# Two sets of raw-weight buffers in a dense FFN, and partition sums by block transpose, row sum and a narrow product

## The chip, the cores and the metric

The kernel runs on 1 core of one Trainium2 chip. The metric is the device time of one execution in microseconds (us). Before the change the median of 3 runs is 1362.73 us (1361.41 to 1363.16).

## What is computed

Two layers over 256 latent tokens of width 1024. Layer 0 is windowed attention (with 256 context tokens as extra keys) and a dense SwiGLU FFN; layer 1 is a pooling mixer and a top-2-of-8 expert FFN. Each sub-layer takes shift, scale and gate vectors from adaLN, a vector-matrix product with a large matrix:

```python
def ada_mod(cond, w, b):
    m = jax.nn.silu(cond) @ w + b
    return jnp.split(m[..., None, :], 6, axis=-1)

def swiglu(h, w_gu, w_down):
    g, u = jnp.split(h @ w_gu, 2, axis=-1)
    return (jax.nn.silu(g) * u) @ w_down

h = modulate(rmsnorm(x, g_pre_ffn), sh_f, sc_f)
f = swiglu(h, ffn_w_gu[slot], ffn_w_down[slot])
x = x + gt_f * rmsnorm(f, g_post_ffn)
```

All is float32. `D_MODEL` is 1024, `D_FF` 2816, `D_FF_EXPERT` 3584.

## The kernel before

The program is written engine by engine; each engine runs its own list in order and waits on semaphores.

**The dense FFN** goes through its 2816 inner columns in 11 steps of 256 (`FSTEPS`, `FS`). A step has three raw weight tiles of 1 MB: f_raw0 and f_raw1 (gate and up columns for the first and the second half of the 1024 inputs) and f_raw2 (256 rows of the down matrix). SyncE (SP) asks for them in `dense_step`. To multiply in full precision each raw tile is split: ScalarE writes a rounded copy f_hi (`dense_hi`, L1177), VectorE the rest f_lo = f_raw - f_hi (`dense_lo`, L1548). TensorE runs per step `gate_up` (48 matmuls on three pairs of parts, L823 to L825), the turn of the last step's activations (L856), one `column_sums` (L660), and `down` of the last step (24 matmuls, L871). In iteration `st` ScalarE does: turned activations of st-1, f_hi0 of st+1, SiLU of st, f_hi1 of st+1, f_hi2 of st. VectorE does: fT_lo of st-1 (L1580), f_lo0 of st+1, the gate product f_act (L1589), f_lo1 of st+1, f_lo2 of st, `take_columns`, and an adaLN piece (`sum_piece`). f_hi and f_lo have one buffer for each of the three kinds, so f_hi2 is written when `down` has read it (semaphore f_used2).

Before the change f_raw too has one buffer for each kind. SP asks for a step's tile when VectorE has split the last step's (f_split0 to f_split2), and its waits stand in one line: f_raw0 and f_raw1 of the next step come behind f_raw2 of this one.

**adaLN.** The matrices have 24 pieces of 512 columns. After the first four, a piece is taken by VectorE: with rows on partitions it scales and adds eight 128x512 chunks into ada_acc (L1414, L1417, `sum_chunk`), which leaves 128 partial sums for each column. `column_sums` adds them up over the partitions on TensorE: four products with a 128-column block of ada_acc as the stationary operand and one column of ones as the moving one, each two records in the profile. `take_columns` (L1408) adds the bias. Pieces 0 to 5 (`MIXER_PIECES`) are taken during the projections; 6 to 9 during attention, a chunk per head on VectorE, and TensorE takes the column sums at heads 10, 18, 26 and after the last; from 10 (`EARLY`) on, one piece in each FFN step 0 to 9, so that its column sums come in the next. GpSimd asks for the pieces.

**Attention** goes over 32 heads-and-blocks `u`: TensorE computes scores of u (L733 to L735), turns the probabilities of u-2 (L744) and weighs the values of u-3 (L755); VectorE takes the maximum (L1510), ScalarE the exponential (L1145).

**The experts' stage** (TensorE L1029 and L1043) begins after the pooling mixer and the router. SP loads its weights (`load`, L410) into five 28 KB-per-partition buffers that begin at SBUF offset R0, where q_parts and the raw FFN tiles lie before.

Of the kernel before, what the change touches and what calls it, by code (L numbers as in the profile page):

```python
# [44 lines left out]
FF = 2816  # L45
FS = 256
# [6 lines left out]
UNIT = 32  # L53
# [80 lines left out]
def build(nc, x, c, ctx_in, c_ctx, ada_w, ada_b, norm_g, w_qkv, w_o, sink, pool_w, pool_b, pool_scale,  # L134
# [4 lines left out]
    def sb(name, shape, dt, at):  # L139
        return nc.alloc_sbuf_tensor_at(name, [shape[0], *shape[1:]], dt, offset=base + at)  # L140
# [155 lines left out]
    def bank(i):  # L296
        return ps[:, i, :]

    names = """x_in ctx_in wqkv_in0 wqkv_in1 wqkv_in2 consts_in tr2_hi mask_r_ready ada_summed ada_rows_taken rows_in sink_in rb_in wo_in ada_in0 ada_in1 ada_in2 ada_fourth_in ada_late_in
        pool_in cols_turned cols_ready silu_ready ada_used acc_ready colsum_ready mod_ready a_ready nsink_ready  # L300
# [4 lines left out]
        f_in0 f_in1 f_in2 f_split0 f_split1 f_split2 f_hi0 f_hi1 f_hi2 f_used0 f_used1 f_used2  # L305
        f_silu f_act_ready f_turned f_thi f_tlo hf_hi_ready hf_ready
# [50 lines left out]
    def _(sp):  # L357
# [18 lines left out]

        def dense_step(st):

            for k in range(2):
                if not isinstance(st, int):  # L380
                    sp.wait_ge(s[f"f_split{k}"], st)
                for half, at in ((0, 0), (1, FF)):
                    sp.dma_start(f_raw[k][:, :, half * FS:half * FS + FS],
                                 gu_v[:, 4 * k:4 * k + 4, bass.ds(st * FS + at, FS)]).then_inc(s[f"f_in{k}"], 16)
            if not isinstance(st, int):
                sp.wait_ge(s["f_split2"], st)
            sp.dma_start(f_raw[2][:], dn_v[bass.ds(st, 1)].rearrange("a p q n -> p (a q) n")
                         if not isinstance(st, int) else dn_v[st]).then_inc(s["f_in2"], 16)
# [206 lines left out]
    def _(pe):  # L595
# [472 lines left out]
    def _(act):  # L1068
# [96 lines left out]

        def dense_hi(k, st):

            act.wait_ge(s[f"f_in{k}"], (st + 1) * (32 if k < 2 else 16))
            if k == 2 and isinstance(st, int) and st == FSTEPS - 1:
                act.wait_ge(s["f_used0"], FSTEPS)  # L1170
                act.activation(last_hi[:], f_raw[k][:], ACT.Copy).then_inc(s["f_hi2"], 1)
# [5 lines left out]
            act.activation(f_hi[k][:], f_raw[k][:], ACT.Copy).then_inc(s[f"f_hi{k}"], 1)  # L1177

        load_table(ACT.Sqrt, 4)
        dense_hi(0, 0)  # L1180
        for b in range(TB):
            act.wait_ge(s["wo_ready"], 2 * b + 2)
            y = ps[:, 3 + 2 * b:5 + 2 * b, :]
            if b == 1:
                act.wait_ge(s["y_normed"], 1)
            squares(NORM_Y + 2 * b, [(y, y_tmp[:].rearrange("p (a n) -> p a n", a=2))])
            root(NORM_Y + 2 * b)
            if b == 1:
                dense_hi(1, 0)
# [21 lines left out]

        def dense_iteration(st, first=False, last=False):
            if not first:
                dense_turned_hi(st - 1)
            if not last:
                dense_hi(0, st + 1)
            dense_silu(st)
            if not last:
                dense_hi(1, st + 1)
            dense_hi(2, st)  # L1220

        dense_iteration(0, first=True)
        with act.Fori(1, FSTEPS - 1) as st:
            dense_iteration(st)
        dense_iteration(FSTEPS - 1, last=True)
        dense_turned_hi(FSTEPS - 1)

# [102 lines left out]
    def _(dve):  # L1330
# [17 lines left out]
        def inverse_root(n):  # L1348
# [61 lines left out]
        def sum_chunk(q, w, k):  # L1410

            v, acc_q = cols[:, N_SC + 2 * k:N_SC + 2 * k + 1], acc_of(q)
            if k == 0:
                ins = dve.tensor_scalar(acc_q[:], w[:, k, :], v, None, ALU.mult)  # L1414
            else:
                dve.wait_ge(s["acc_ready"], q * KC + k)
                ins = dve.scalar_tensor_tensor(acc_q[:], w[:, k, :], v, acc_q[:], ALU.mult, ALU.add)  # L1417
            ins.then_inc(s["acc_ready"], 1)

        def sum_piece(q, w):  # L1420
            for k in range(KC):
                sum_chunk(q, w, k)
# [84 lines left out]
        for u in range(NU):  # L1507
# [35 lines left out]

        def dense_lo(k, st):
# [54 lines left out]
        dense_iteration(0, first=True)  # L1599
        with dve.Fori(1, FSTEPS - 1) as st:  # L1600
            dense_iteration(st)
        dense_iteration(FSTEPS - 1, last=True)
        dense_turned_lo(FSTEPS - 1)
# [246 lines left out]
```

## Time and profile before

| | before |
|---|---|
| median of 3 runs | 1362.73 us |
| the profiled execution, its own time | 1363.89 us |
| its span, first to last instruction | 1362.2 us |
| TensorE busy | 1210.1 us, 89% |
| VectorE busy | 579.1 us, 43% |
| ScalarE busy | 315.5 us, 23% |
| mean granted TensorE clock | 0.955 |
| bytes moved | 461.20 MB, 339 GB/s over the span |
| dense FFN, first to last matmul | about 220 to 430 us |
| experts' first matmul | 489.65 us |

Busy times are unions over the span. PE is TensorE's matmuls, PEld its weight loads, DVE VectorE, ACT ScalarE, POOL GpSimd, SP SyncE. A busy TensorE in the profile is one with a matmul in its pipeline.

### The profile page before, as it was taken

To read this page: it belongs to the slowest core of one execution; us is meant where nothing else is said; L and a number is where in the kernel's file an instruction comes from. 1 tells how busy PE (TensorE), PEld (TensorE's weight loads), DVE (VectorE), ACT (ScalarE), POOL (GpSimd) and SP (SyncE) were. 2 spreads that over 40 slices of the span, in tenths; PEclk is the share of its full clock that TensorE was granted. 3 is DMA by queue.
4 is the path that set the end of the run, shared out by engine and by line. 5 is a ranking of instruction groups with operands and counts; after the bars stand their busy time and mean duration, and the time that the engine had idled before them with its cause. 6 is when DMAs were issued, how large, how long until landed. Compare 5 with 4: busy or idle time off the path is not lost.

```text
span 1362.2 us, 43494 instructions
## 1 busy us (share of the span) xinstructions
PE 1210.1 (89%) x16960; PEld 850.3 (62%) x16960; DVE 579.1 (43%) x1117; ACT 315.5 (23%) x535; POOL 168.3 (12%) x517
## 2 busy tenths in 40 slices
PE   3898998999999999989979899878989976999971
PEld 1456975788888676656647566546755644766751
DVE  0597845777776543232323233312432321323322
ACT  2005653334343422111102012011111100211111
POOL 1010000000010011111111111111111110111111
PEclk9899999999999999999989899989999988999996
DMA  9995120588899458899999999999999999999995
GB/s 336 390 367 191 63 93 32 192 293 291 303 324 403 190 210 347 331 410 414 412 411 411 402 412 411 412 415 410 411 412 413 411 411 412 413 373 411 414 406 180
DMA packets 129077, 461.20 MB, mean 339 GB/s; under 512 B 8240, under 2 KB 34016, under 8 KB 120672
## 3 DMA queue, kind: packets, MB, share of 16 engines
q1 hardware_dynamic: 114368, 403.78, 75.4%
q0 software_dynamic: 13952, 55.58, 11.0%
q8 instruction: 74, 1.21, 0.4%
q10 hardware_dynamic: 672, 0.54, 0.2%
q14 instruction: 11, 0.09, 0.0%
HBM read 455.81 MB, written 4.06 MB: 338 GB/s over the span
## 4 chain that ended last, share of the span: by engine, by line
PE 66%; DMA 15%; SPq 8%; DVE 4%; issue 4%; ACT 1%; POOL 0%; POOLq 0%; DVEq 0%; ACTq 0%
PE ps L1029 28%; PE ps L1043 13%; DMA w_gu<-in_moe_w_gu 8%; SPq L410 8%; PE ps L871 4%; PE ps L695 4%; PE ps L823 2%; PE ps L824 2%; PE ps L825 2%; DMA ctx_tok<-in_ctx 2%; PE ps L813 2%; PE ps L755 2%; DMA w_dn<-in_moe_w_down 1%; DMA ada<-in_ada_w 1%; DMA f_raw<-in_ffn_w_gu 1%
## 5 line engine op out<-in xcount | busy, mean ns | idle before, releaser
L1029 PE MATMUL ps<-w_gu,x_cur 128*32 128x224 f32 x10240 | 514.0, 363 | 61.6 <-issue 29.9
L1029 PEld LDWEIGHTS ps<-w_gu,x_cur 128*32 128x32 f32 x10240 | 362.8, 113 | 209.5 <-issue 74.8
L1043 PE MATMUL ps<-w_dn,consts_sb 128*32 128x256 f32 x4480 | 258.8, 385 | 20.1 <-POOL consts_sb L548 10.1
L1761 DVE TENSOR_TENSOR cols<-cols,ps 128x224 f32<-128x224 f32 x160 | 91.7, 573 | 416.7 <-PE ps L1029 416.7
L1043 PEld LDWEIGHTS ps<-w_dn,consts_sb 128*32 128x32 f32 x4480 | 151.8, 111 | 121.0 <-issue 34.7
L1289 ACT ACTIVATE cols<-ps 128x224 f32<-128x224 f32 x160 | 93.4, 584 | 561.3 <-PE ps L1029 433.3
L1417 DVE SCALAR_TENSOR_TENSOR ada_acc<-ada,cols,ada_acc 128x512 f32<-128x512 f32 x140 | 105.0, 750 | 4.0
L1548 DVE TENSOR_TENSOR f_lo<-f_raw,f_hi 128x2048 fp32r<-128x2048 f32 x32 | 73.0, 2292 | 48.1 <-ACT f_hi L1177 46.9
L537 POOL COPY x_cur<-x_all 128x128 f32 x160 | 47.7, 298 | 317.4 <-PE ps L1029 271.0
L1177 ACT ACTIVATE f_hi<-f_raw 128x2048 fp32r<-128x2048 f32 x32 | 61.0, 1916 | 65.9 <-DMA f_raw<-in_ffn_w_gu 60.7
L823 PE MATMUL ps<-f_hi,hf_hi 128*128 128x512 f32 x176 | 71.5, 406 | 2.7 <-DVE f_act L1589 2.7
L539 POOL COPY x_cur<-x_all 128x128 f32 x160 | 47.4, 296 | 181.2 <-PE ps L1029 181.2
L824 PE MATMUL ps<-f_lo,hf_hi 128*128 128x512 f32 x176 | 69.7, 396 | 0.0
L825 PE MATMUL ps<-f_hi,hf_lo 128*128 128x512 f32 x176 | 69.6, 395 | 0.0
L1304 ACT ACTIVATE kept<-cols 128x224 f32 x80 | 31.2, 390 | 145.1 <-DVE cols L1761 145.1
L1788 DVE TENSOR_TENSOR y_all<-y_all,ps 128x256 f32 x60 | 25.3, 422 | 78.7 <-PE ps L1043 68.1
L1791 DVE TENSOR_TENSOR y_all<-y_all,ps 128x256 f32 x80 | 33.7, 422 | 56.0 <-PE ps L1043 56.0
L548 POOL COPY consts_sb<-kept 128x128 f32 x80 | 23.7, 296 | 177.7 <-DVE kept L1776 108.0
L695 PE MATMUL ps<-wqkv,hT 128*128 128x512 f32 x96 | 44.1, 613 | 1.1 <-DVE hT L1388 1.1
L823 PEld LDWEIGHTS ps<-f_hi,hf_hi 128*128 128x128 f32 x176 | 33.7, 191 | 10.6 <-issue 3.2
L513 POOL DMA_DIRECT2D ada<-in_ada_w x10 | 8.9, 885 | 251.8 <-DVE ada_acc L1417 251.8
L825 PEld LDWEIGHTS ps<-f_hi,hf_lo 128*128 128x128 f32 x176 | 33.8, 192 | 7.4
(246 smaller groups left out, 1067.6 us busy)
## 6 DMA issues: line engine op xcount, KB each, us to landing
w_gu<-in_moe_w_gu SPq DMA_DIRECT2D x256, 896.0 KB
w_dn<-in_moe_w_down SPq DMA_DIRECT2D x32, 2048.0 KB
w_dn<-in_moe_w_down SPq DMA_DIRECT2D x32, 1536.0 KB
ada<-in_ada_w POOLq DMA_DIRECT2D x23, 2048.0 KB, 10.1
f_raw<-in_ffn_w_gu SPq DMA_DIRECT2D x44, 512.0 KB, 6.7
f_raw<-in_ffn_w_down SPq DMA_DIRECT2D x11, 1024.0 KB, 4.9
wqkv<-in_attn_w_qkv SPq DMA_DIRECT2D x3, 2048.0 KB, 19.6
wo_sb<-in_attn_w_o SPq DMA_DIRECT2D x1, 4096.0 KB, 23.6
```

The lines of the kernel that those rows point to most:

```text
L410: sp.dma_start(to, src).then_inc(s[f"w_{x}{part // 2}"], 32 if kind == DOWN else 16)
L695: mm = pe.matmul(bank(3 + u % 4), src[:, k, b * P:(b + 1) * P], wqkv[:, k, 512 * n:512 * n + 512], start=(k == 0), stop=(k == KC - 1))
L823: pe.matmul(bank(1 + b), hi, f_hi[k][:, kk, :], start=first, stop=False)
L824: pe.matmul(bank(1 + b), hi, f_lo[k][:, kk, :], start=False, stop=False)
L825: mm = pe.matmul(bank(1 + b), lo, f_hi[k][:, kk, :], start=False, stop=last)
L1029: mm = pe.matmul(ps[UNIT * t:UNIT * t + UNIT, bank_, 0:W], x_cur[:, k, :], w_gu[x][:, k, W * t:W * t + W], start=(k % 4 == 0), stop=(k % 4 ...
L1043: mm = pe.matmul(ps[UNIT * t:UNIT * t + UNIT, bank_, 0:OW], act_cur[:, q, :], w_dn[x][:, q, OW * t:OW * t + OW], start=(q == rows[0]), sto ...
L1177: act.activation(f_hi[k][:], f_raw[k][:], ACT.Copy).then_inc(s[f"f_hi{k}"], 1)
L1289: act.activation(halves.rearrange("p (q c) -> p c q", q=MQ), ps[:, HALF_BANK, 0:W].rearrange("p (c q) -> p c q", q=MQ), ACT.Copy).then_inc ...
L1417: ins = dve.scalar_tensor_tensor(acc_q[:], w[:, k, :], v, acc_q[:], ALU.mult, ALU.add)
L1548: dve.tensor_tensor(lo[:], f_raw[k][:], hi[:].bitcast(F32), ALU.subtract).then_inc(s[f"f_split{k}"], 1)
L1761: dve.tensor_tensor(view, view, ps[:, REST_BANK, 0:W].rearrange("p (c q) -> p c q", q=MQ), ALU.add).then_inc(s["rest_taken"], 1)
```

## The change

1. f_raw gets two sets ("sides") of three tiles. Side 0 lies where the tiles lay, side 1 at R0, over q_parts and two small attention tiles. Step st uses side st mod 2. SP asks for step 0 as before, for step 1 when attention's output is taken (o_taken 4) and adaLN pieces to 9 are done (mod_ready), and for step st from 2 on when the tiles of step st-2 are split. Loops of SP, ScalarE and VectorE take two steps an iteration. The experts' first three quarter chunks lie under side 1 and now wait for the splits of step 9.
2. For adaLN pieces from 6 on, VectorE turns ada_acc in 32x32 blocks (`gather_rows`: transpose, then a sum over the 32 elements of each row), which leaves 4x4 values on each partition; TensorE multiplies them with a 128x32 pattern of ones (`fold_all`, made once by a row sum) in four narrow products, one for each 32 partitions of the output.

```diff
-    f_raw = [sb(f"f_raw{k}", [P, 4, 2 * FS] if k < 2 else [P, 2, D], F32, R0 + 24 * KB + 8 * KB * k)
-             for k in range(3)]
+    f_raw = [[sb(f"f_raw{k}{side}", [P, 4, 2 * FS] if k < 2 else [P, 2, D], F32, R0 + 24 * KB * (1 - side) + 8 * KB * k)
+              for side in range(2)] for k in range(3)]
...
+        def dense_step(st, side):
+            fixed = isinstance(st, int)
             for k in range(2):
+                if not fixed:
+                    sp.wait_ge(s[f"f_split{k}"], st - 1)
...
+            if not fixed:
+                sp.wait_ge(s["f_split2"], st - 1)
...
         sp.wait_ge(s["qkv_ready"], 8)
-        dense_step(0)
-        with sp.Fori(1, FSTEPS) as st:
-            dense_step(st)
+        dense_step(0, 0)
+        sp.wait_ge(s["o_taken"], 4)
+        sp.wait_ge(s["mod_ready"], EARLY)
+        dense_step(1, 1)
+        with sp.Fori(0, FSTEPS // 2 - 1) as i:
+            for side in range(2):
+                dense_step(i * 2 + (2 + side), side)
+        sp.wait_ge(s["f_split0"], FSTEPS - 2)
+        sp.wait_ge(s["f_split1"], FSTEPS - 2)
+        sp.wait_ge(s["f_split2"], FSTEPS - 2)
...
+        for k in range(3):
+            sp.wait_ge(s[f"f_split{k}"], FSTEPS - 1)
         load(0, GATE, 0, 0, (0, 1, 2))
...
         def column_sums(q):
+            if not isinstance(q, int) or q >= MIXER_PIECES:
+                pe.wait_ge(s["acc_rows_ready"], q - MIXER_PIECES + 1)
+                pe.wait_ge(s["mod_ready"], q)
+                for t in range(TILES):
+                    mm = pe.matmul(ps[UNIT * t:UNIT * t + UNIT, 0, 0:4], fold_all, acc_rows[:, t, :], start=True, stop=True)
+                mm.then_inc(s["colsum_ready"], 1)
+                return
...
+        done(dve.tensor_reduce(fold_all, ident.rearrange("p (j a) -> p a j", a=UNIT), AX.X, ALU.add), step_, wait=False)
...
+        def gather_rows(q):
+            n = q - MIXER_PIECES
+            dve.wait_ge(s["acc_ready"], (q + 1) * KC)
+            dve.transpose(acc_turned[:].rearrange("p a b -> p (a b)"), acc_of(q)[:]).then_inc(s["acc_turned_ready"], 1)
+            dve.wait_ge(s["acc_turned_ready"], n + 1)
+            dve.tensor_reduce(acc_rows[:].rearrange("p t k -> p k t"), acc_turned[:].rearrange("p (k t) b -> p k t b", t=TILES),
+                              AX.X, ALU.add).then_inc(s["acc_rows_ready"], 1)
...
+            if u % KC == 0 and u:
+                gather_rows(MIXER_PIECES + u // KC - 1)
...
+        gather_rows(EARLY - 1)
         take_columns(EARLY - 1)
...
                 sum_piece(st + EARLY, ada_ring[0])
+                gather_rows(st + EARLY)
```

VectorE at the end of FFN step 0 and the head of the next, before the change (f_lo_78 and f_lo_79 are the low parts of kinds 1 and 2):

```order
L1548 TENSOR_TENSOR f_lo_78<-f_raw_64,f_hi_75 128x2048 [waits f_hi1]
L1548 TENSOR_TENSOR f_lo_79<-f_raw_65,f_hi_76 128x2048 [waits f_hi2]
L1414 TENSOR_SCALAR ada_acc_92<-ada_70,cols 128x512 [waits ada_late_in]
L1417 SCALAR_TENSOR_TENSOR ada_acc_92<-ada_70,cols,ada_acc_92 128x512 [waits acc_ready] x7
L1600 UNCONDITIONAL_BRANCH
L1580 TENSOR_TENSOR fT_lo<-ps,fT_hi 128x512 [waits f_thi]
```

and now:

```order
L1592 TENSOR_TENSOR f_lo_81<-f_raw_66,f_hi_78 128x2048 [waits f_hi1]
L1592 TENSOR_TENSOR f_lo_82<-f_raw_67,f_hi_79 128x2048 [waits f_hi2]
L1446 TENSOR_SCALAR ada_acc_95<-ada_73,cols 128x512 [waits ada_late_in]
L1449 SCALAR_TENSOR_TENSOR ada_acc_95<-ada_73,cols,ada_acc_95 128x512 [waits acc_ready] x7
L1456 STREAM_TRANSPOSE acc_turned<-ada_acc_95 128x512 [waits acc_ready]
L1458 TENSOR_REDUCE acc_rows<-acc_turned 128x4x4 [waits acc_turned_ready]
L1624 TENSOR_TENSOR fT_lo<-ps,fT_hi 128x512 [waits f_thi]
```

The two new instructions stand between the piece's sum and fT_lo, as in every step up to the ninth.

SP's requests from the FFN's first on, before (f_raw_63 to f_raw_65 are kinds 0 to 2):

```order
L383 DMA f_raw0_63<-in_ffn_w_gu 128x4x256 [waits qkv_ready]
L383 DMA f_raw0_63<-in_ffn_w_gu 128x4x256
L383 DMA f_raw1_64<-in_ffn_w_gu 128x4x256 x2
L387 DMA f_raw2_65<-in_ffn_w_down 128x2x1024
L392 UNCONDITIONAL_BRANCH
L383 ISA [waits f_split0]
L383 DMA f_raw0_63<-in_ffn_w_gu 128x4x256
```

and now (the last digit of f_raw00 or f_raw01 is the side):

```order
L388 DMA f_raw00_63<-in_ffn_w_gu 128x4x256 [waits qkv_ready]
L388 DMA f_raw00_63<-in_ffn_w_gu 128x4x256
L388 DMA f_raw10_65<-in_ffn_w_gu 128x4x256 x2
L392 DMA f_raw20_67<-in_ffn_w_down 128x2x1024
L388 DMA f_raw01_64<-in_ffn_w_gu 128x4x256 [waits mod_ready,o_taken]
L388 DMA f_raw01_64<-in_ffn_w_gu 128x4x256
L388 DMA f_raw11_66<-in_ffn_w_gu 128x4x256 x2
L392 DMA f_raw21_68<-in_ffn_w_down 128x2x1024
L400 UNCONDITIONAL_BRANCH
```

Step 1's four requests stand ahead of the loop, behind a wait of their own.

## Rows read from the trace of the kernel before

**Rows 1.** The page's slices of the span: DMA engines' busy share in tenths.
```profile
DMA  9995120588899458899999999999999999999995
```

**Rows 2.** Chain of waits in order of time: start us, us, what.
```profile
249.86 10.97 DMA f_raw<-in_ffn_w_gu
...
489.65 10.40 PE ps L1029 x213
```

**Rows 3.** Timeline, one FFN step: start us, us, engine, line, operation, count, [idle before, releaser].
```profile
298.18 0.39 PE L823 MATMUL ps<-f_hi,hf_hi 128*128 128x512 f32 x1
...
310.76 1.92 ACT L1177 ACTIVATE f_hi<-f_raw 128x2048 fp32r<-128x2048 f32 x1 [5.90 <-DMA f_raw<-in_ffn_w_gu]
...
315.95 0.39 PE L823 MATMUL ps<-f_hi,hf_hi 128*128 128x512 f32 x1
...
316.21 1.92 ACT L1177 ACTIVATE f_hi<-f_raw 128x2048 fp32r<-128x2048 f32 x1 [0.53 <-PE ps L871]
...
318.16 2.29 DVE L1548 TENSOR_TENSOR f_lo<-f_raw,f_hi 128x2048 fp32r<-128x2048 f32 x1 [0.15 <-ACT f_hi L1177]
...
320.95 5.47 DVE L1417 SCALAR_TENSOR_TENSOR ada_acc<-ada,cols,ada_acc 128x512 f32<-128x512 f32 x7
...
327.30 0.94 PE L660 MATMUL ps<-consts_sb,ada_acc 128*128 128x1 f32 x8
...
328.11 0.72 PE L871 MATMUL ps<-f_hi,fT_hi 128*128 128x512 f32 x2
```

**Rows 4.** Timeline of FFN steps 1 to 3.
```profile
261.79 0.39 PE L823 MATMUL ps<-f_hi,hf_hi 128*128 128x512 f32 x1
...
262.80 4.49 DVE L1548 TENSOR_TENSOR f_lo<-f_raw,f_hi 128x2048 fp32r<-128x2048 f32 x2 [1.47 <-ACT f_hi L1177]
...
267.79 5.48 DVE L1417 SCALAR_TENSOR_TENSOR ada_acc<-ada,cols,ada_acc 128x512 f32<-128x512 f32 x7
...
273.40 1.05 PE L660 MATMUL ps<-consts_sb,ada_acc 128*128 128x1 f32 x8
...
280.33 0.47 PE L823 MATMUL ps<-f_hi,hf_hi 128*128 128x512 f32 x1 [0.29 <-DVE f_act L1589]
```

**Rows 5.** Timeline of attention heads 8 to 11, and of the stage's end.
```profile
138.38 0.47 PE L733 MATMUL ps<-k_hi,q_parts 128*128 128x512 f32 x1
...
140.23 0.47 PE L733 MATMUL ps<-k_hi,q_parts 128*128 128x512 f32 x1
...
142.98 0.47 PE L733 MATMUL ps<-k_hi,q_parts 128*128 128x512 f32 x1
...
143.78 0.69 DVE L1510 TENSOR_REDUCE small<-ps 128x1 f32<-128x512 f32 x1 [1.14 <-PE ps L735]
...
188.28 0.16 DVE L1408 TENSOR_TENSOR cols<-ps,cols 128x4 f32<-128x4 f32 x1 [3.84 <-PE ps L660]
```

**Rows 6.** VectorE's groups by form: count, busy us, mean ns, idle before.
```profile
L1417 DVE SCALAR_TENSOR_TENSOR ada_acc<-ada,cols,ada_acc 128x512 f32<-128x512 f32 x140 | 105.0, 750 | 4.0
...
L1774 DVE STREAM_TRANSPOSE actT<-cols 128x224 f32<-128x224 f32 x80 | 32.9, 412 | 2.7
...
L1510 DVE TENSOR_REDUCE small<-ps 128x1 f32<-128x512 f32 x32 | 22.0, 688 | 7.6 <-PE ps L735 7.4
```

**Rows 7.** Timeline of weight loads at the router's logits.
```profile
467.05 0.38 PEld L980 LDWEIGHTS ps<-hr,route_wide 128*32 128x32 f32 x16 [0.81 <-DVE hr L1682]
467.62 0.30 PEld L961 LDWEIGHTS ps<-consts_sb 128*128 128x128 f32 x2 [0.20 <-issue]
```

**Rows 8.** Timeline, TensorE at the last step's down.
```profile
424.19 0.70 PE L871 MATMUL ps<-down_last_hi,fT_hi 128*128 128x512 f32 x2 [0.84 <-ACT fT_hi L1207]
```

**Rows 9.** Timeline at step 1, and a stretch: busy us by engine, PEclk, DMA.
```profile
242.32 0.47 PE L823 MATMUL ps<-f_hi,hf_hi 128*128 128x512 f32 x1 [2.36 <-DVE f_act L1589]
...
244.00:246.00 2.00, 2.00 (x6) 1.62 (x5) 2.00 (x2) 0.19 (x1) 0.00 (x0) 0.50 0.00 0
```

More of the change, by code:

```diff
@@ L202, in build @@
     g_row = sb("g_row", [P, D], F32, S[0])
+    acc_turned = sb("acc_turned", [P, 16, 32], F32, S[0] + 4 * KB)
+    acc_rows = sb("acc_rows", [P, 4, 4], F32, S[0] + 6 * KB)
     y_tmp = sb("y_tmp", [P, D], F32, S[0] + 4 * KB)
@@ L241, in build @@
     ones = ct[:, K_ONE:K_ONE + P]
+    fold_all = cols[:, 416:416 + UNIT]
     def cos_of(b):
@@ L299, in build @@
     names = """x_in ctx_in wqkv_in0 wqkv_in1 wqkv_in2 consts_in tr2_hi mask_r_ready ada_summed ada_rows_taken rows_in sink_in rb_in wo_in ada_in0 ada_in1 ada_in2 ada_fourth_in ada_late_in
-        pool_in cols_turned cols_ready silu_ready ada_used acc_ready colsum_ready mod_ready a_ready nsink_ready
+        pool_in cols_turned cols_ready silu_ready ada_used acc_ready acc_turned_ready acc_rows_ready colsum_ready mod_ready a_ready nsink_ready
         sumsq_ready msq_ready sqrt_ready rstd_ready dve_step xn_ready turn_ready turned_taken
@@ L304, in build @@
         row_ready row_taken wo_ready y_normed
-        f_in0 f_in1 f_in2 f_split0 f_split1 f_split2 f_hi0 f_hi1 f_hi2 f_used0 f_used1 f_used2
+        f_in00 f_in01 f_in10 f_in11 f_in20 f_in21 f_split0 f_split1 f_split2 f_hi0 f_hi1 f_hi2 f_used0 f_used1 f_used2
         f_silu f_act_ready f_turned f_thi f_tlo hf_hi_ready hf_ready
@@ L375, in _ @@
         sp.dma_start(wo_sb[:], w_o[0].rearrange("(k p) n -> p k n", p=P)).then_inc(s["wo_in"], 16)
-        def dense_step(st):
+        def dense_step(st, side):
+            fixed = isinstance(st, int)
             for k in range(2):
-                if not isinstance(st, int):
-                    sp.wait_ge(s[f"f_split{k}"], st)
+                if not fixed:
+                    sp.wait_ge(s[f"f_split{k}"], st - 1)
                 for half, at in ((0, 0), (1, FF)):
[L383 to L388, printed above, removed]
@@ L390, in _ @@
-        sp.wait_ge(s["qkv_ready"], 8)
-        dense_step(0)
-        with sp.Fori(1, FSTEPS) as st:
-            dense_step(st)
+                    sp.dma_start(f_raw[k][side][:, :, half * FS:half * FS + FS],
+                                 gu_v[:, 4 * k:4 * k + 4, bass.ds(st * FS + at, FS)]).then_inc(s[f"f_in{k}{side}"], 16)
+            if not fixed:
+                sp.wait_ge(s["f_split2"], st - 1)
+            sp.dma_start(f_raw[2][side][:], dn_v[st] if fixed else dn_v[bass.ds(st, 1)].rearrange("a p q n -> p (a q) n")
+                         ).then_inc(s[f"f_in2{side}"], 16)
@@ new lines, in _ @@
+        sp.wait_ge(s["qkv_ready"], 8)
+        dense_step(0, 0)
[8 more added lines that the diff above has]
+        sp.wait_ge(s["f_split2"], FSTEPS - 2)
+        assert FSTEPS % 2 == 1
+        for k in range(2):
+            for half, at in ((0, 0), (1, FF)):
+                sp.dma_start(f_raw[k][0][:, :, half * FS:half * FS + FS],
+                             gu_v[:, 4 * k:4 * k + 4, (FSTEPS - 1) * FS + at:FSTEPS * FS + at]).then_inc(s[f"f_in{k}0"], 16)
@@ L395, in _ @@
+        sp.dma_start(f_raw[2][0][:], dn_v[FSTEPS - 1]).then_inc(s["f_in20"], 16)
         GATE, UP, DOWN = range(KINDS)
@@ L1164, in _, with dense_hi @@
         take_row(g_row, (0, 7), 0)
-        def dense_hi(k, st):
-            act.wait_ge(s[f"f_in{k}"], (st + 1) * (32 if k < 2 else 16))
+        def dense_hi(k, st, side, turn):
+            act.wait_ge(s[f"f_in{k}{side}"], (turn + 1) * (32 if k < 2 else 16))
             if k == 2 and isinstance(st, int) and st == FSTEPS - 1:
                 act.wait_ge(s["f_used0"], FSTEPS)
-                act.activation(last_hi[:], f_raw[k][:], ACT.Copy).then_inc(s["f_hi2"], 1)
+                act.activation(last_hi[:], f_raw[k][side][:], ACT.Copy).then_inc(s["f_hi2"], 1)
                 return
@@ L1176, in dense_hi @@
                 act.wait_ge(s[f"f_used{k}"], st)
-            act.activation(f_hi[k][:], f_raw[k][:], ACT.Copy).then_inc(s[f"f_hi{k}"], 1)
+            act.activation(f_hi[k][:], f_raw[k][side][:], ACT.Copy).then_inc(s[f"f_hi{k}"], 1)
         load_table(ACT.Sqrt, 4)
-        dense_hi(0, 0)
+        dense_hi(0, 0, 0, 0)
         for b in range(TB):
@@ L1210, in _, with dense_iteration @@
         take_row(g_row, (0, 7), 2)
-        def dense_iteration(st, first=False, last=False):
+        def dense_iteration(st, side, turn, first=False, last=False):
+            ahead = (1 - side, turn + side)
             if not first:
@@ L1215, in dense_iteration @@
             if not last:
-                dense_hi(0, st + 1)
+                dense_hi(0, st + 1, *ahead)
             dense_silu(st)
             if not last:
[L1219 to L1225, printed above, removed]
+                dense_hi(1, st + 1, *ahead)
+            dense_hi(2, st, side, turn)
+        dense_iteration(0, 0, 0, first=True)
+        dense_iteration(1, 1, 0)
+        with act.Fori(0, FSTEPS // 2 - 1) as i:
+            for side in range(2):
+                dense_iteration(i * 2 + (2 + side), side, i + 1)
+        dense_iteration(FSTEPS - 1, 0, FSTEPS // 2, last=True)
         dense_turned_hi(FSTEPS - 1)
@@ L1542, in y_flat, with dense_lo @@
             return v if len(v.shape) == 2 else v.rearrange("p a n -> p (a n)")
-        def dense_lo(k, st):
+        def dense_lo(k, st, side):
             dve.wait_ge(s[f"f_hi{k}"], st + 1)
             hi, lo = (last_hi, last_lo) if k == 2 and isinstance(st, int) and st == FSTEPS - 1 else (f_hi[k], f_lo[k])
-            dve.tensor_tensor(lo[:], f_raw[k][:], hi[:].bitcast(F32), ALU.subtract).then_inc(s[f"f_split{k}"], 1)
+            dve.tensor_tensor(lo[:], f_raw[k][side][:], hi[:].bitcast(F32), ALU.subtract).then_inc(s[f"f_split{k}"], 1)
         dve.wait_ge(s["row_taken"], 2)
-        dense_lo(0, 0)
+        dense_lo(0, 0, 0)
         for b in range(TB):
@@ L1555, in _ @@
             if b == 1:
-                dense_lo(1, 0)
+                dense_lo(1, 0, 0)
             inverse_root(NORM_Y + 2 * b + 1)
@@ L1581, in dense_turned_lo, with dense_iteration @@
                               fT_hi[:].rearrange("p q b t -> p (q b t)").bitcast(F32), ALU.subtract).then_inc(s["f_tlo"], 1)
-        def dense_iteration(st, first=False, last=False):
+        def dense_iteration(st, side, first=False, last=False):
             if not first:
@@ L1586, in dense_iteration @@
             if not last:
-                dense_lo(0, st + 1)
+                dense_lo(0, st + 1, 1 - side)
             dve.wait_ge(s["f_silu"], st + 1)
@@ L1590, in dense_iteration @@
             if not last:
-                dense_lo(1, st + 1)
-            dense_lo(2, st)
+                dense_lo(1, st + 1, 1 - side)
+            dense_lo(2, st, side)
             if not first:
@@ L1597, in dense_iteration @@
                 sum_piece(st + EARLY, ada_ring[0])
[L1599 to L1602, printed above, removed]
+                gather_rows(st + EARLY)
+        dense_iteration(0, 0, first=True)
+        dense_iteration(1, 1)
+        with dve.Fori(0, FSTEPS // 2 - 1) as i:
+            for side in range(2):
+                dense_iteration(i * 2 + (2 + side), side)
+        dense_iteration(FSTEPS - 1, 0, last=True)
         dense_turned_lo(FSTEPS - 1)
```

2 lines of the change are left out of this document (1 added, 1 removed).

## The prediction

> **What bounds the kernel now.** I read the page's slices first. From the eighteenth slice on the DMA engines stand at nine tenths and more [rows 1]: that is the experts' stage, which streams 3.67 MB chunks through five buffers as TensorE frees them. Nothing of it is edited. Its first buffers fill long before TensorE arrives, and each later load waits for a freed buffer, so a stage before it that ends 1 us sooner moves TensorE's start, the freeing and the last byte 1 us sooner. I count whatever happens before 489 us at full value.
>
> The chain of waits in order of time comes next, for the dense FFN between 220 and 430 us. It runs through a raw-weight DMA of 10.97 us near 250 us, and reaches the experts' first matmul at 489.65 [rows 2]. So a late raw tile is on the path early in this stage; whether it is in its steady part is for the timeline.
>
> Step to step the first `gate_up` matmul goes from 298.18 to 315.95: 17.77 us. ScalarE does wait 5.90 us for raw weights before its copy at 310.76 [rows 3], which is the wait that the change is to remove, but TensorE has no gap. The step is TensorE's own sum: column sums start at 327.30, 11.35 us after the step's start; `down` starts 0.81 us later, and the next step 5.61 us after that [rows 3].
>
> Beside it runs a second round that nearly closes too. When `down` has read f_hi2, ScalarE refills it (316.21, 0.26 us after the step's start), VectorE splits it (318.16) and then sums the adaLN piece until 320.95 + 5.47 = 326.42, which is 10.47 us into the step [rows 3]. Only then may TensorE take the column sums. Released in 0.13 us (267.79 + 5.48 = 273.27, matmul at 273.40 [rows 4]) this round would allow 10.60 us; TensorE arrives at 11.35. **The slack is 0.75 us**, and the second part of the change puts two VectorE instructions into just this round.
>
> **The change, part by part.** *Raw weights in two sets.* The same bytes move through the same queue: each step SP still issues five DMAs when f_split2 lets it go, but for tiles needed one step later. ScalarE's f_hi0 copy will follow the turned activations at once, up to 5.90 us earlier. Steady gain for TensorE: 0, since it did not wait. f_hi2 does not move: it waits for `down`, not for data. SP now waits for o_taken and mod_ready before step 1's loads; behind it stand only FFN loads, and they go out near 190 us, when the DMA is nearly idle, and are used after 237. The experts' first three quarter chunks wait for the splits of step 9 (side 1 lies under them). In the order of the rows that is the very split that released them before: 0. The last step's raw `down` comes earlier, but TensorE there waits 0.84 us for ScalarE's turned activations [rows 8], so 0. If this cover went, the price would be 0.84 us at most.
>
> *What VectorE gains as work.* A block transpose of 512 columns and a row sum of 512. The transpose is in the trace with 224 columns at 0.412 us, the row sum with 512 (from PSUM) at 0.688 [rows 6]. VectorE's slope is (2.29 - 0.75) / 1536 = 1.0 ns per column (f_lo with 2048 columns [rows 3], the adaLN step with 512 [rows 6]), so the transpose is 0.412 + 0.29 = 0.70. Dependent instructions follow each other after 0.04 us (seven adaLN steps of 0.75 take 5.47). Together 0.04 + 0.70 + 0.04 + 0.69 = **1.47 us**. Bounds: 1.2 (row sum from SBUF cheaper) and 2.0 (it takes its 4x4x32 view more slowly). I take the middle, as both rows are of the same engine and nearly the same shape.
>
> *What TensorE loses as work.* Four products with a 128-column stationary operand, eight records, 0.81 us between neighbours here [rows 3] and 0.90 in attention: a head that has them takes 142.98 - 140.23 = 2.75 us, one that has not 140.23 - 138.38 = 1.85 [rows 5]. The new ones have a 32-column stationary operand and four moving columns. The router's logits are the nearest rows: 16 such loads in 0.38 us, about 0.02 each, then 0.20 us of idle before the next full-width load [rows 7]. So 8 x 0.02 + 0.20 = **0.38 us** from the first to `down`. The entry into the narrow form is in no row free of other waits: 0 to 0.20; I take 0.17, 0.55 in all where TensorE arrives without a wait. The Trainium skill (TensorEngine Tiling (Array Packing), Key Properties) says that changing the tiling mode, not just the tile, drains TensorE. By this rule the way out costs the 0.20 us that the row shows, in the sum above; without it the products would be 0.16 us everywhere and the change some 3 us better.
>
> *Attention, pieces 6 to 9.* Four column sums, 0.90 - 0.55 = 0.35 us each. The fourth stands in front of the last VectorE chain of the stage, which waits 3.84 us for it [rows 5], so all four count: **-1.4 us** (bounds -2.6 and 0). VectorE's 1.47 us fall behind heads 8, 16 and 24. VectorE idles 1.14 us before the maximum of the head whose scores stand behind the column sums [rows 5], with less before each head until then, and the probabilities are turned two heads after their scores, 3.7 us. This covers 1.47 us barely; if the cover were gone, up to 0.5 us each, 1.5 in all.
>
> *FFN, beginning.* Step 1's column sums find the sums ready, so 0.26 us is saved and step 2 starts at 261.53 instead of 261.79 [rows 4]. In step 2 f_hi1 was late for want of raw weights, and f_lo2 with it (262.80 x2, 4.49 us to 267.29). Now f_lo2 ends at 261.53 + 0.26 + 1.92 + 0.03 + 2.29 = 266.03 and the sum 5.98 later at 272.01; column sums at 272.01 + 1.47 + 0.13 = 273.61, step 3 at 273.61 + 0.38 + 5.61 = 279.60. It was 280.33 [rows 4]: **-0.7 us**. This is all that the second buffer set earns.
>
> *FFN, steady.* Column sums start at 10.47 + 1.47 + 0.13 = 12.07 us into the step. Plus 0.38 and 5.61: 18.06, against 17.77: +0.29 a step. Over the seven steps from 3 to 10 and the column sums of step 10, 8 x 0.29 = **+2.3 us**. Behind the new pair on VectorE stand fT_lo (`down` needs it about 0.9 us into its run; it ends 0.7 us after the pair), f_lo0 and f_act, which end some 3 us after that (0.7 + 2.29 + 0.7 after the pair's 11.94), at 15.6 of 18.06. None is late.
>
> *Start.* One more row sum, 128 columns, while VectorE idles: 0.
>
> **Sum:** -1.4 - 0.7 + 2.3 = +0.2 us. The profiled execution's own 1363.89 us becomes 1364.1. It lay 1.2 us above the median of the three runs, so against 1362.73 I predict **1362.9 us**. A measurement of this kernel can tell about 0.2%, 2.7 us, from no change.
>
> **Rivals.**
> A. *The VectorE round sets the step* (above): 1362.9, own range 1360.5 to 1365.5. Chance 0.56.
> B. *The narrow products cost next to nothing*: 0.20 in all. Attention -2.8, beginning -1.1, step 12.07 + 0.20 + 5.61 = 17.88, +0.9 in eight: -3.0, so 1359.7. For it: 0.02 us a load [rows 7]. Against: the 0.20 us of idle in the same rows. Chance 0.14.
> C. *TensorE stays the bound.* If the pair took under 0.75 us, or f_hi2 came sooner, the step would be 17.77 - 0.43 = 17.34: -3.4, with attention and beginning -5.5, so 1357.2. Against: f_hi2 hangs on `down`, and the row sum's row alone is 0.69. Chance 0.06.
> D. *Slower: the VectorE round is longer than I sum.* It decides from about 1.8 us for the pair on, since each 0.1 us costs 0.8. The likeliest way is a row sum that takes two slots of 1.0 ns for each of its 512 columns, as it walks them in short rows: 0.51 us more, a pair of 1.98, a step of 18.57, 8 x 0.51 = 4.1 us more, +4.3 in all, so 1367.0. For it: no row has such a view or a row sum of this width from SBUF. Against: VectorE's rows of 512 and 2048 columns keep one slope. Chance 0.18. The Trainium skill (VectorE: DVE Perf Modes, The DRAIN you can't avoid) names another way: a flush behind each operation of its duration less 266 ns, which would put an estimated 0.43 us behind the transpose and give 1366.3. The trace speaks against that one, with seven adaLN steps of 0.75 us that follow each other after 0.04 [rows 3, 6].
> E. *TensorE's clock falls at the new wait* of 12.07 - 11.35 = 0.7 us a step. After TensorE's idle 2.36 us before 242.32 the granted clock was 0.50 from 244 to 246, that is 1.2 GHz [rows 9]; 2 us at half speed lose 1, in every step 8 us, 1371. Against: the wait of 0.84 us at 424.19 [rows 8] was followed by two matmuls in 0.70 us, no more than the 0.72 at 328.11 [rows 3]. Chance 0.03.
> F. *The buffers don't do what they say*, f_hi0 still late: the beginning gains nothing, 1363.6. Chance 0.03; the SP rows speak against it.
>
> **The numbers.** 1362.9 is A's. Faster by over 0.2% (below 1360.0): C, most of B, an edge of A: 0.20. Slower by over 0.2% (above 1365.4): most of D, E: 0.18. Same: 0.62. The range of 1359.0 to 1367.0 holds A, B and most of D; C and E stay out.
>
> **What would show it.** ScalarE's wait for raw weights, 5.90 us in the step shown, gone but for the last step; TensorE waiting 0.6 to 0.8 us in each FFN step for acc_rows; a steady step of 18.0 to 18.1; transpose 0.70 and row sum 0.69 us; heads with column sums at 2.4 instead of 2.75 us; the first experts' matmul within 1 us of 489.65. I am wrong if the step is under 17.8 (B, C) or over 18.3 (D, E), or if a head after a VectorE pair is late.

## The result, and the profile after

| | before | changed |
|---|---|---|
| median of 20 runs each, same chip | 1363.59 us | 1361.62 us |
| ratio, 95% interval | | 0.9983 (0.9975 to 0.9991) |
| profiled execution, own time and span | 1363.89, 1362.2 us | 1361.92, 1360.2 us |
| TensorE, VectorE busy | 1210.1, 579.1 us | 1201.8, 596.2 us |
| experts' first matmul | 489.65 us | 487.56 us |

The change gains 0.17%, 2.3 us with an interval of 1.2 to 3.4. The forecast was 0.2 us of loss, so it is off by 2.5 us and wrong in sign. That the median lies in the range of 1359.0 to 1367.0 says little: the range is 8 us wide and holds no change at all. A ratio is always to runs of the kernel before on the same chip; other tables compare single executions by their traces.

One FFN step of the changed kernel, from its timeline (start us, us, engine, line, operation, count, idle before), answers to [rows 3]:

```profile
313.97 1.92 ACT L1204 ACTIVATE f_hi<-f_raw 128x2048 fp32r<-128x2048 f32 x1 [4.12 <-PE ps L898]
...
324.22 0.71 DVE L1456 STREAM_TRANSPOSE acc_turned<-ada_acc 128x512 f32<-128x512 f32 x1
324.97 0.69 DVE L1458 TENSOR_REDUCE acc_rows<-acc_turned 128x16 f32<-128x512 f32 x1
...
325.57 0.68 DVE L1624 TENSOR_TENSOR fT_lo<-ps,fT_hi 128x512 fp32r<-128x512 f32 x1
...
325.79 0.24 PE L678 MATMUL ps<-acc_rows,cols 128*32 128x4 f32 x8 [0.56 <-DVE acc_rows L1458]
...
325.96 0.73 PE L898 MATMUL ps<-f_hi,fT_hi 128*128 128x512 f32 x2
```

This step starts at 313.71 and the next at 331.56: 17.85 us. ScalarE now waits for TensorE (4.12 us), no longer for raw weights. The pair takes 0.71 and 0.69 us. TensorE waits 0.56 us for it and takes the products 12.08 us into the step. From there to `down` are 0.17 us. (The profile counts the 0.56 us from where it shows the last matmul ending. That one starts at 324.84 and the next would start 0.23 us later, at 325.07, so the products come 0.72 us later than they could.)

The table of waits of the changed kernel, 215 to 440 us (engine, line, waited for: us, times, longest):

```profile
PE ps L678 <- DVE acc_rows L1458: 4.9, 9, 0.6
...
ACT f_hi L1204 <- DMA f_raw<-in_ffn_w_gu: 3.8, 2, 3.2
```

In the kernel before ScalarE waited 60.7 us, 18 times, for raw gate and up weights here. The first line is the new wait: nine times 0.5 to 0.6 us. The last line is step 9, where ScalarE waits for the last step's weights.

Attention's head with column sums, in TensorE's timeline, and the end of the stage on VectorE, answer to [rows 5]:

```profile
140.53 0.47 PE L760 MATMUL ps<-k_hi,q_parts 128*128 128x512 f32 x1
...
142.51 0.24 PE L678 MATMUL ps<-acc_rows,cols 128*32 128x4 f32 x8
142.68 0.50 PE L760 MATMUL ps<-k_hi,q_parts 128*128 128x512 f32 x1
...
186.29 0.16 DVE L1440 TENSOR_TENSOR cols<-ps,cols 128x4 f32<-128x4 f32 x1 [1.73 <-PE ps L678]
```

Such a head takes 142.68 - 140.53 = 2.15 us instead of 2.75, so the sums cost 0.30 us over a plain head's 1.85. VectorE's chain at the end starts 1.99 us sooner.

**Where the time went.** Cut at five places of TensorE's timeline, for nine of the runs (us, as differences of starts; the steps by their first `gate_up` matmul):

| run | first head to FFN | FFN to step 2 | step 2 to 3 | mean of next 7 | step 10 to experts |
|---|---|---|---|---|---|
| before | 96.65 | 41.31 | 18.54 | 17.79 | 84.82 |
| before_again | 96.67 | 39.68 | 17.85 | 17.82 | 84.72 |
| changed | 94.37 | 41.71 | 17.85 | 17.83 | 84.68 |
| after_again | 94.38 | 40.75 | 17.83 | 17.83 | 84.67 |
| e1_buffers | 96.64 | 39.68 | 17.76 | 17.76 | 84.67 |
| e2_sums | 94.71 | 40.58 | 19.01 | 17.85 | 84.71 |
| e3_sums_after_down | 94.37 | 40.61 | 17.27 | 17.27 | 83.92 |
| e4_both_later | 94.36 | 40.63 | 17.21 | 17.20 | 83.84 |
| e8_later_one_raw_set | 94.38 | 41.09 | 19.25 | 17.55 | 83.97 |

Changed less before: -2.28, +0.40, -0.69, 7 x 0.045 = +0.32 and -0.14; the first head was 0.30 later. Together -2.09 us, as at the experts' first matmul. The two profiled once more differ by -2.29, +1.07, -0.02, +0.12, -0.05. Only the first column is stable: attention earns 2.3 us. The second and third vary with the execution, and the rest is some tenths. The second column's higher numbers are no cost of the change: e6 and e7 (below), which have its buffers and its sums, take 39.44 and 39.58 us there, no more than the 39.68 of before_again.

### The profile page after: what moved, and what is told of

Same layout as the page of the kernel before. It is cut to its first block, busy times and chain, and to the rows that moved or that the text cites. A ratio compares the mean times of both kernels' runs of the same rounds, so it can differ in the third digit from the quotient of the medians.

```text
span 1360.2 us, 43450 instructions
## 1 busy us (share of the span) xinstructions
PE 1201.8 (88%) x16960; PEld 841.1 (62%) x16960; DVE 596.2 (44%) x1146; ACT 314.7 (23%) x535; POOL 166.8 (12%) x517
## 4 chain that ended last, share of the span: by engine, by line
PE 60%; DMA 11%; DVE 10%; SPq 10%; issue 6%; ACT 2%; DVEq 0%; POOL 0%; POOLq 0%; ACTq 0%
PE ps L1056 28%; PE ps L1070 12%; SPq L428 9%; DMA w_gu<-in_moe_w_gu 6%; PE ps L898 5%; PE ps L722 4%; DVE ada_acc L1449 4%; PE ps L840 2%; PE ps L782 2%; DMA wqkv<-in_attn_w_qkv 2%; DMA w_dn<-in_moe_w_down 1%; ACT f_hi L1204 1%; DMA ada<-in_ada_w 1%; PE ps L771 1%; PE ps L760 1%
```

## The experiments

**Each part alone, and each kernel once more.** e1 is the changed kernel with the old column sums for all pieces:

```diff
-            if not isinstance(q, int) or q >= MIXER_PIECES:
+            if False:
```

and without its three `gather_rows` calls and `fold_all`.

> The kernel before with the two sets of raw buffers alone; the column sums of all pieces stay as they were. Theory (the buffers earn only the late raw tile of the second step): steady step 17.77 us as before, step 2 starts at 261.79, step 3 at 261.79 + 17.77 = 279.56 instead of 280.33, the last step as before: 0.8 us faster than before in all, ratio 0.9994. Rival (the buffers earn most of the change's 2.3 us): 2 us faster or more, ratio 0.9985, with a shorter steady step or a shorter last step. Second rival (they do nothing): ScalarE still waits for raw weights, ratio 1.0000.

e2 is the kernel before with everything of the sums (`gather_rows` and its calls, the narrow products, `fold_all`) and one set of raw tiles.

> The kernel before with the new partition sums alone; one set of raw buffers. Theory (the narrow products are cheap, the VectorE round sets the FFN step): attention 4 x 0.6 = 2.4 us shorter; step 3 at 273.27 + 1.47 + 0.13 + 0.17 + 5.61 = 280.65 less what attention saved; steady step 17.85; the clock at half speed near 228 to 232 us costs 0.95 us if it belongs to the earlier end of attention. Together -2.4 + 0.3 + 0.6 + 0.95 = -0.6 us against before, ratio 0.9996; -1.5 us and 0.9989 if the clock's loss is an accident of one execution. Rival (the sums cost as much in the FFN as they save in attention and the buffers earn all): ratio 1.000 to 1.001, FFN step over 18.0.

e1: 1362.37 against 1363.44 us, ratio 0.9991 (0.9982 to 1.0001). e2: 1360.87 us, 0.9986 (0.9975 to 0.9997). The measurement can part e1 neither from no change nor, as its interval reaches 0.9982, from the whole 2.3 us. Its trace says where it could gain: in step 3, and in steady steps that stay at 17.76 without the jitter of the two profiles of before, where the mean is 17.79 and 17.82. e2 has attention's gain and a steady step of 17.85, as forecast; its step 3 starts late for raw weights (19.01). The rival that the buffers earn most of it falls by the traces: attention takes 96.64 us in e1 as before, and 94.71 in e2.

> The kernel before once more, for its profile alone. Theory (where TensorE's clock falls between 226 and 250 us differs from one execution to the next): from the first head to the first gate_up 96.65 us as before, but from the first gate_up to step 2 another time than 41.31, anywhere from 39.7 to 41.8. Rival (the clock's stretches belong to the kernel): 41.3 again within 0.1.

> The changed kernel once more, for its profile alone. Theory (the same): first head to first gate_up 94.4 us, steady step 17.83 to 17.85, and from the first gate_up to step 2 another time than 41.71, anywhere from 39.4 to 41.8. Rival (the clock's stretches belong to the kernel, and take 1 us of what attention saves): 41.7 again within 0.1.

They came out at 1362.09 and 1362.42 us, one execution each. From the first `gate_up` to step 2 the kernel before took 39.68 instead of 41.31 us, the changed one 40.75 instead of 41.71. The windows show why (us, busy us by engine, PEclk, DMA). In the kernel before the granted clock is 0.76 from 242 to 244 us and 0.50 in the next two [rows 9]; in before_again:

```profile
242.00:244.00 2.00, 1.04 (x5) 0.90 (x6) 1.75 (x3) 2.00 (x2) 0.00 (x0) 1.00 0.00 0
244.00:246.00 2.00, 2.00 (x11) 1.65 (x9) 2.00 (x2) 0.84 (x1) 0.00 (x0) 1.00 0.00 0
```

The same wait of 2.36 us for f_act is followed by half the clock (1.2 GHz) in one execution and by the full one (2.4 GHz) in the other. The two profiles of the changed kernel differ at the stretch before, behind a wait of 3.50 us for xn: the granted clock is 0.50 from 226 to 232 us in one, and 0.84, 0.50 and 0.80 in the other. It is an accident of the execution, 1 to 1.6 us large, in a measurement that is to show 2. The late step 3 of [rows 4] is another: here is its cause, a late raw tile, the first row from the kernel before, the second from before_again.

```profile
275.34 1.92 ACT L1177 ACTIVATE f_hi<-f_raw 128x2048 fp32r<-128x2048 f32 x1 [6.87 <-DMA f_raw<-in_ffn_w_gu]
```

```profile
273.49 1.92 ACT L1177 ACTIVATE f_hi<-f_raw 128x2048 fp32r<-128x2048 f32 x1 [5.90 <-DMA f_raw<-in_ffn_w_gu]
```

Where ScalarE waits 6.87 us for the raw tile, step 2 to 3 takes 18.54 us; where it waits 5.90, 17.85. That wait shows in TensorE's own at step 3's start (0.29 us, for f_act [rows 4]); another 0.15 us were lost before, as the column sums of step 2 start 11.61 us into it (273.40 - 261.79 [rows 4]) and 11.46 in before_again.

**What sets the step of 17.85 us.** e7 makes the row sum of each FFN piece twice, into a place `acc_again` first:

```diff
+            if not isinstance(q, int) or q >= EARLY:
+                dve.tensor_reduce(acc_again[:].rearrange("p t k -> p k t"), ...)
             dve.tensor_reduce(acc_rows[:].rearrange("p t k -> p k t"), ...
```

> The changed kernel with VectorE's row sum of each FFN piece made twice, the first into a place that nobody reads. Theory (the VectorE round sets the step of 17.85 us): the whole 0.69 to 0.73 us comes on top, step 18.54 to 18.58, 5.5 to 5.8 us in eight steps. Rival (TensorE's own work or the products' price sets the step, VectorE has slack): step under 18.2.

```profile
324.40 0.69 DVE L1460 TENSOR_REDUCE acc_again<-acc_turned 128x16 f32<-128x512 f32 x1
325.00 0.68 DVE L1462 TENSOR_REDUCE acc_rows<-acc_turned 128x16 f32<-128x512 f32 x1
...
325.81 0.24 PE L679 MATMUL ps<-acc_rows,cols 128*32 128x4 f32 x8 [1.15 <-DVE acc_rows L1462]
```

The step is 18.42 us (mean of seven), 0.59 longer, and TensorE's wait grows from 0.56 to 1.15, by the same 0.59. VectorE's round sets the step. My 0.69 to 0.73 was too much: the two row sums, which don't depend on each other, start 0.60 us apart (324.40, 325.00) although they are shown with 0.69 and 0.68. (e7, as e5, e6, e9 and e10 below, is one execution, read by its trace.)

e3 puts the column sums behind `down`, in the loop and likewise in the first and last step:

```diff
-            column_sums(st + EARLY - 1)
             down(st - 1)
+            column_sums(st + EARLY - 1)
```

> The changed kernel, with TensorE's column sums of each FFN step behind that step's down products instead of ahead of them. Theory (TensorE waits in each step for VectorE's rows): the wait for acc_rows is gone; down now waits for fT_lo, which VectorE makes 0.7 us behind the pair, about 0.2 to 0.4 us late, so a step of 17.45 to 17.65 against 17.85, 2 to 3 us faster than the change, ratio to before 0.9960 to 0.9970. Rival (the wait only moves in full, VectorE's round stays the bound through fT_lo): step 17.8 to 17.9, ratio 0.998. Rival (TensorE's own sum is already the bound at 17.85): step 17.85 or more.

e4 in addition makes fT_lo ahead of the pair:

```diff
                 dense_turned_lo(st - 1)
+                gather_rows(st + EARLY - 1)
...
                 sum_piece(st + EARLY, ada_ring[0])
-                gather_rows(st + EARLY)
```

> As the run with the column sums behind down, and VectorE makes fT_lo before the transpose and row sum instead of behind them. Theory (the VectorE round is then 1.47 us shorter than TensorE's): TensorE has no wait in the steady step, which is 17.77 - 0.81 + 0.17 to 0.30 = 17.13 to 17.26 us; 8 x 0.6 to 0.7 = 5 us faster than the change, 7 us faster than before, ratio 0.9945 to 0.9955. Rival (another wait takes its place at once, such as f_lo0 or the silu's product, 1.5 us later on VectorE): step 17.5 or more, ratio 0.997.

e3: 1356.06 us, ratio 0.9947 (0.9932 to 0.9962), step 17.27. e4: 1355.06 us, 0.9937 (0.9921 to 0.9952), step 17.20. The wait of 0.56 us is gone in both. In e3 `down` waits 0.2 us for fT_lo. My 17.45 to 17.65 was high because f_hi2 is now refilled at the step's very start (328.68, the step from 328.69), not 0.26 us into it (313.97 against 313.71 in the changed kernel), which I had not counted. In e4 TensorE waits for nothing in a steady step. The last step gives 0.84 us more (the table's last column), which my 0.9945 to 0.9955 left out: its column sums now stand where TensorE waited for fT_hi. e4 beats the changed kernel (its ratio, 0.9937, lies below 0.9983, and the intervals don't overlap) by some 6.3 us.

e8 is e4's order with one set of raw tiles.

> The run with both the column sums and the rows later, with one set of raw buffers as before the change. Theory (the second set hides a wait that a shorter step would lay bare): f_hi0 lands 8 us after f_split2 lets it go, f_lo0 ends 16.7 us into the step and the silu's product 17.3, against a step of 17.20 that they must not pass, so a step of 17.25 to 17.4; with step 3, which was 0.7 to 1.2 us late, 1 to 3 us slower than with two sets, ratio to before 0.994 to 0.996. Rival (the raw loads' round is far from the bound, the second set earns nothing): ratio 0.9937 as with two sets. Rival (the shorter step asks for more bytes per us than the queues give, and the round closes at 17.7): ratio 0.9965.

1359.76 us, ratio 0.9969 (0.9959 to 0.9979). Its timeline:

```profile
345.08 1.92 ACT L1188 ACTIVATE f_hi<-f_raw 128x2048 fp32r<-128x2048 f32 x1 [5.75 <-DMA f_raw<-in_ffn_w_gu]
...
350.06 0.47 PE L834 MATMUL ps<-f_hi,hf_hi 128*128 128x512 f32 x1 [0.26 <-DVE f_act L1614]
```

TensorE waits at each step's start for f_act (349.23), which stands behind f_lo0 (347.02), which stands behind the late raw tile. The raw weights' round closes at 17.4 to 17.7 us, 17.55 in the mean: below the 17.8 of the two kernels, so that it hid there, and above e4's 17.20. The second buffer set is worth 0.4 us by the ratios in the change as made (0.9986 of e2 less 0.9983), far within the noise, and 4.4 us once the column sums are out of the way (0.9969 - 0.9937; the intervals don't overlap). My 17.25 to 17.4 was low and the rival's 17.7 high for the step; by the ratio the rival's 0.9965 fits and my 0.994 to 0.996 doesn't. The profile is of e8's slowest execution, 1362.11 us, where its twelve range from 1354.65 to 1362.11, so the mean step of the others may be shorter.

**What the narrow products cost.** All four start from e4, where TensorE has no wait, so that its step shows a cost whole. e5 issues the FFN's products four times over (`for _ in range(4)` around them).

> The run with both the column sums and the rows later (TensorE without a wait, step 17.20 us), but each FFN step issues its four narrow products four times over, 32 records instead of 8; the output is the same. Theory (0.02 us a record, and a small price for going in): 24 more records add 0.5 us, step 17.7. Rival (the price is in entering or leaving the narrow form, the records themselves are free): step under 17.3. Rival (each product costs a drain of its own, as the 0.38 us of the prediction would be if spread over its records, 0.05 a record): step 18.3 or more.

e6 splits them:

```diff
-            down(st - 1)
-            column_sums(st + EARLY - 1)
+            down(st - 1, parts=(0,))
+            column_sums(st + EARLY - 1, range(2))
+            down(st - 1, parts=(1,))
+            column_sums(st + EARLY - 1, range(2, TILES))
```

> The same kernel with step 17.20 us, but two of the four narrow products stand between the two halves of down and two behind it, so that TensorE goes into the narrow form and out of it twice a step instead of once. Theory (going in costs about 0.08 us, going out nothing): step 17.25 to 17.30. Rival (the prediction's prices, 0.17 in and 0.20 out, or any drain at a change of form of that size): step 17.57. Rival (no price at all): 17.20.

e9 leaves the FFN's products out (`pe.sem_inc(s["colsum_ready"], 1)` in their place), and with them those pieces' columns.

> The run with both the column sums and the rows later (TensorE without a wait, step 17.20 us), with the four narrow products of each FFN step left out, so that those pieces' columns are not computed; all waits and VectorE's work stay. Theory (one visit to the narrow form costs a busy TensorE 0.36 us whatever the number of products: 0.09 in, 0.17 inside, 0.10 for the next full-width load): step 16.84. Rival (only the 0.17 us inside are paid): step 17.03. Rival (without the products another round is the bound, VectorE's or the raw weights'): step over 17.1.

e10 gives them `ident` as stationary operand and all 128 output rows.

> The same kernel with step 17.20 us, with a 128-column stationary operand (the identity) in the place of the 32-column one in each FFN step's four products, still four moving columns; those pieces' columns come out as something else. Theory (the load of 128 columns is what the old sums paid, 0.10 us a record): eight records in 0.81 us instead of 0.17, step 17.84. Rival (going into the narrow form is what costs, and a full-width product of four columns is as cheap as a narrow one): step 17.1 to 17.3.

| | step, us | against e4 |
|---|---|---|
| e9, none | 16.80 | -0.40 |
| e4, 8 narrow records at one place | 17.20 | |
| e6, 4 and 4, at two places | 17.57 | +0.37 |
| e5, 32 at one place | 17.64 | +0.44 |
| e10, 8 full-width records at one place | 17.76 | +0.56 |

The steps are means of the seven from step 3 to step 10. Only the steps of e9 and e10 are compared, not their whole times, as their wrong columns change what the router does later. TensorE's weight loads in e4, then loads and matmuls in e10:

```profile
328.23 0.16 PEld L678 LDWEIGHTS ps<-acc_rows,cols 128*32 128x32 f32 x8 [0.35 <-issue]
328.40 0.19 PEld L850 LDWEIGHTS ps<-f_hi,hf_hi 128*128 128x128 f32 x1
```

```profile
329.38 1.08 PEld L679 LDWEIGHTS ps<-acc_rows,consts_sb 128*128 128x128 f32 x8
329.60 0.95 PE L679 MATMUL ps<-acc_rows,consts_sb 128*128 128x4 f32 x8
...
330.41 0.49 PE L853 MATMUL ps<-f_hi,hf_hi 128*128 128x512 f32 x1
```

A full-width load goes 0.22 us ahead of its own matmul, beneath the last one. The narrow load stands idle for 0.35 us and goes at the same time as its matmul. The 0.40 us of a visit in e4 are made up like this: `down`'s last pair starts at 327.69, and pairs follow each other there after 0.46, so the first product could start at 328.15 and does at 328.23 (0.08); the next full-width matmul starts 0.18 later (328.41); and the one behind that after 0.33 instead of 0.23 (0.10). That is 0.36; where the other 0.04 go is not shown.

e6 refutes my "going in costs about 0.08, going out nothing": a second visit costs 0.37, nearly as much as e4's one, though each has only four records. In e6's timeline four records take 0.16 us to the next full-width matmul, hardly less than eight do in e4 (0.18):

```profile
324.60 0.23 PE L678 MATMUL ps<-acc_rows,cols 128*32 128x4 f32 x4
324.76 0.73 PE L899 MATMUL ps<-f_hi,fT_hi 128*128 128x512 f32 x2
```

e5 seems to give the record itself 0.44 / 24 = 0.018 us, near the 0.02 of [rows 7], but its timeline parts this in two. First a visit at a turn of the loop, then the one ahead of the loop:

```profile
329.06 0.43 PE L679 MATMUL ps<-acc_rows,cols 128*32 128x4 f32 x32
329.73 0.47 PE L851 MATMUL ps<-f_hi,hf_hi 128*128 128x512 f32 x1 [0.23 <-issue]
```

```profile
258.60 0.43 PE L679 MATMUL ps<-acc_rows,cols 128*32 128x4 f32 x32
259.01 0.47 PE L851 MATMUL ps<-f_hi,hf_hi 128*128 128x512 f32 x1
```

The idle of 0.23 to 0.26 us stands behind the seven visits from which the loop goes back to its start. The visit ahead of the loop and the one from which it is left (399.74, next matmul 400.19) have none, and take 0.41 and 0.45 us. Against e4's 0.18 the 24 records more cost 0.23 to 0.27 us, about 0.01 each; the rest of e5's 0.44 goes with the loop's turn. Why eight records don't bring that idle out in e4 is not shown.

By the Trainium skill (TensorEngine Tiling (Array Packing), Key Properties) a change of mode drains TensorE. The trace agrees in so far as the narrow load is not taken ahead and the first product comes 0.08 us late, while e10's full-width ones come on time (329.14 to 329.60, 0.46); no run separates a drain from another cause of the 0.08. The 0.10 behind is no part of it, since e10's full-width products have it too (its first three matmuls behind them start at 330.41, 330.73 and 330.97). e10's records are 0.10 us each (330.41 - 329.60 = 0.81), exactly what the old sums took [rows 3]: it was the 128-column loads that they paid. My 17.84 for e10 left out that its products don't pay the 0.08 ahead.

## Why the prediction was right and wrong

- **The VectorE round sets the FFN step: right.** Products forecast 12.07 us into the step, measured 12.08; transpose 0.70 and row sum 0.69 against 0.71 and 0.69; e7 adds to the round and the step follows, e3 and e4 take the wait away and it falls to TensorE's own sum. The waits forecast (0.6 to 0.8 a step for acc_rows, ScalarE's raw wait gone but for the last step) are there at 0.56 in the profile's count, 0.72 from where TensorE could have gone on, and 3.8 us.
- **The step that failed is the price of the narrow products**, "8 x 0.02 + 0.20 = 0.38 us from the first to `down`", 0.55 with the way in. Measured: 0.17 from the first to `down`, and 0.30 in all in an attention head, in the terms in which the old sums cost 0.90. I took the 0.20 us idle behind the router's sixteen loads [rows 7] for a fixed price of the way out. In the changed kernel no idle stands there, and in e5 none stands behind 32 narrow records either, except at a turn of the loop. So the way out has no such price; what makes the idle at the router stays open.
- **What this term did to the sum.** Steady FFN: 8 x (0.38 - 0.17) = 1.7 us, so +0.6 instead of +2.3. Attention: 4 x (0.55 - 0.30) = 1.0, so -2.4 instead of -1.4. It stands in the beginning too, in step 1's column sums (0.25) and ahead of step 3 (0.21): -1.2 instead of -0.7. Together -3.0, against -2.3 (1.2 to 3.4) measured. It is the sum of rival B (0.20 in all, step 17.88, attention -2.8), whose mechanism the runs bear out for the change as made (a busy TensorE pays more, e9) and which I gave 0.14.
- **Attention** earned 2.28 us of the 2.4 that four times 0.60 make; the other 0.12 are not placed. No head behind a VectorE pair came late; VectorE's 1.14 us of slack and the two heads' lead took the pair up, as forecast. The forecast sign, heads at 2.4 us, was missed with the price (2.15), and so was the experts' first matmul within 1 us of 489.65 (487.56).
- **FFN, beginning**, forecast -0.7: the rows from which I worked it out were one execution's accident (step 2 to 3 took 18.54 us, 17.85 in the other). That the changed kernel has just -0.69 there is luck: against the second profile of before it has -0.02. The whole beginning, to step 3, differs by -0.29 us in one pair of profiles and by +1.05 in the other, with the clock's 1 to 1.6 us in it, so what the change earns there is not shown.
- **FFN, steady**: forecast 18.06, measured 17.83 to 17.85; 12.08 + 0.17 + 5.60 makes 17.85, so the products' term alone was wrong. The kernel before is itself at 17.79 to 17.82, with some steps late, so the loss was 0.1 to 0.3 us.
- **Clock** (rival E): the new wait of 0.56 us a step is followed by no fall; the granted clock is 1.00 from 262 to 406 us. The falls near 230 us stand behind a wait of 3.50 us and those near 244 behind one of 2.36, in some executions.
- **Slower** (rival D): the row sum walks its 4x4x32 view at the usual pace (0.69 us), and 0.04 us lie between transpose and row sum. The flush that the Trainium skill (VectorE: DVE Perf Modes, The DRAIN you can't avoid) would have put there does not show: the row sum starts 0.75 us after the start of a transpose of 0.71.

## What to carry to other kernels

When two rounds of waits nearly close together, work out both before moving work between their engines, and move the step that waits behind work that does not need it: the same instructions in another order (e4) gained 6.3 us on top of the change's 2.3. A buffer that seems to earn nothing is to be tried again when the step gets shorter (e8). Price a new instruction form from a place where it stands between the same neighbours, since an idle beside it can belong to something else, and take a term that rests on one late arrival only if a second execution has it too.

## What was not expected of the hardware

- A visit to the 32-column form costs a busy TensorE 0.37 (e6's second) to 0.40 us (e4 against e9) with four records or with eight, and about 0.01 us for each further one (e5). Where TensorE waits for the products anyway, the next full-width matmul starts 0.17 us behind the first of them.
- With 32 narrow records ahead of the loop's turn TensorE idles 0.23 to 0.26 us there; with eight it doesn't (e5, e4).
- VectorE's independent operations of 0.69 us start 0.60 us apart (e7); a row sum that needs the transpose starts 0.74 to 0.75 us after it.
- Whether TensorE's granted clock fell to half behind the same wait differs between two executions of the same kernel, 1 to 1.6 us of its time.
